# Sparse attention two heads ahead: logits, exponentials and a shorter index search in a hybrid encoder layer

## The chip, the cores and the metric

The kernel runs on one core of a Trainium2 chip. The metric is the time of one launch on the device, in microseconds; the kernel before took 3575.22 (median of 3 runs, 3574.49 to 3578.63). The engines are TensorE (PE; its weight loads are PEld), VectorE (DVE), ScalarE (ACT), GpSimd (POOL) and SyncE (SP), which issues the DMAs.

## The reference

One layer of an encoder for 2048 prompt rows and 64 sample rows (behind 512 cached ones), in float32. Normalised rows are projected into queries, keys, values and an indexer; a pooling mixer, a sparse attention (8 heads over 2 key heads, 64 wide) and an attention into 256 memory tokens (4 heads) run side by side; an output projection and a gated feed-forward with a short convolution follow. The change is in the sparse attention:

```python
s = einsum('bthd,bsd->bths', qi, ki)                  # 8 index heads of 32
score = einsum('bth,bths->bts', wi, relu(s))          # one score per query and key
score = where(visible, score, -inf)                   # chunks of 64, causal
top_val, top_idx = top_k(score, top_k)                # 256 keys of a prompt row, 144 of a sample row
...
logits = einsum('btjgd,btnjd->btjgn', qg, k_sel) * HEAD_DIM ** -0.5
p = softmax(where(valid, logits, -inf)); o = einsum('btjgn,btnjd->btjgd', p, v_sel)
```

## The kernel before, in words

The program is a row of stages (memory keys, projection, attention, then output projection and feed-forward in two halves), each ended for all engines before the next begins. The attention stage, `phase_attend`, works on 17 blocks: block n of 0 to 15 has 128 query rows and S = 128(n+1) visible columns, block 16 is the sample (64 rows, 576 columns). Columns are cut into segments of at most 512 (`segs`), tiles of 128, groups of four tiles, and units of two segments. Instead of gathering keys, the kernel finds for each row which columns belong to its largest scores and adds -1e30 to the others' logits.

For each block there are two pieces of work. First the index: TensorE multiplies index queries with index keys, a piece for each of 8 heads and each segment (`index_pieces`, L903, into the two banks of `ps_i`); ScalarE rectifies each (L1030, into a ring of three groups of four); GpSimd weighs, adds up and writes the scores (L877 to L888). VectorE then searches, row by row in parallel, a bound that leaves the wanted number above it (`pick`): it takes the smallest and largest score (L1084, L1085), halves that range 11 times, each time counting the scores above the middle (L1093) and moving it (L1096, L1097), and then takes up to eight more values below the bound by one maximum and one replacement (`take_next`, L1121 to L1124). Where a row needs more than eight, a branch (L1113) takes further rounds, and in the end a general selection by 32 rounds. Blocks 0 and 1 see at most 256 columns and need no search: there are 15.

Then the heads: 8 attention heads and one memory head a block, each a slot. TensorE makes the logits of the first two segments of the next head (`early_logits`, into the two banks of `ps_l`), then turns the present head's probabilities group by group (L946), and multiplies them with the values (L978); segments past the second come in between. VectorE adds the mask to the logits and takes the maximum, one unit at a time (`mask_logits`, L1197); ScalarE takes exponentials (L1038) and copies turned groups back to SBUF (L808); VectorE divides after heads 3, 7 and the memory head (`divide`). The memory head's exponentials are taken by ScalarE straight from `ps_l` (L1042).

The order is written out by hand, one list for each engine, over the same slots. Before the change, in slot h of block n, TensorE makes the logits of head h+1 and a tenth of the index pieces of block n+2 (a fifth in slot 8), ScalarE takes the exponential of head h+1 after all copies of head h, and VectorE does: mask of head h+1 (first unit), division, search part 2h of block n+1, mask (second unit), search part 2h+1. Each engine runs its list in order and waits on semaphores. At a block's first head TensorE waits for the exponentials of the block before, since these read `ps_l`:

```python
if h == 0 and s < 2 and b.n:
    pe.wait_ge(exp_done, NHEADS * b.n)
```

Of the kernel before, what the change touches and what calls it, by code (L numbers as in the profile page):

```python
# [12 lines left out]

# [11 lines left out]
P = 128  # L25
# [12 lines left out]
CHUNK = 64  # L38
# [10 lines left out]
HALVINGS = 11  # L49
FAR = 1.0e30  # L50
NEVER = 1.0e38
RING = 3
UNSEEN, TAKEN, TAKEN_BELOW = -2.0e38, -3.0e38, -2.5e38
# [632 lines left out]
def phase_attend(nc, t, keep):  # L686
# [10 lines left out]
    with ExitStack() as ctx:  # L697
# [9 lines left out]
        probs = m.sb("probs", [P, 2, SEQ])  # L707
# [7 lines left out]
        low, spread, back = m.sb("low", [P, 1]), m.sb("spread", [P, 1]), m.sb("back", [P, 1])  # L715
# [17 lines left out]
        KEY_LOADS, TABLE_LOADS, Q_LOADS = 6, 2, 6  # L733
        SHARE = 10
        NHEADS = NH + 1

# [19 lines left out]

        def slots():

            for b in BLOCKS:
                for h in range(NHEADS):  # L760
                    yield b, h, (b, h + 1) if h + 1 < NHEADS else (None if b.sample else (BLOCKS[b.n + 1], 0))

# [3 lines left out]
        def portion(b, part):  # L766


            total = IH * len(b.segs)
            cut = lambda part: total if part == NHEADS else total * part // SHARE  # L770
            return range(cut(part), cut(part + 1))
# [9 lines left out]
        def copy_groups(act, b, h, late=None):  # L781

            count = len(b.groups) if h < NH else 2
            for g in range(count):
                if g == 1 and late:
                    late()
                    late = None
# [22 lines left out]
            if late:  # L810
                late()
# [4 lines left out]
        def _(sp):  # L816
# [34 lines left out]
            sp.dma_start(places[:, :], t["places"]).then_inc(tables_loaded, 16)  # L851
            load(BLOCKS[1])
# [39 lines left out]
        def _(pe):  # L892
# [24 lines left out]
            def segment_logits(b, h, s):  # L917
# [8 lines left out]
                if h == 0 and s < 2 and b.n:  # L926
                    pe.wait_ge(exp_done, NHEADS * b.n)
# [21 lines left out]
            def head_values(b, h, other, numbers, after):  # L949
# [5 lines left out]
                if h < NH:  # L955
                    groups, src = b.groups, probs[0:T, seq % 2, :]
                else:
                    groups = [[(P * i, P * i + P) for i in range(4 * g, 4 * g + 4)] for g in range(2)]
                    src = probs[0:T, seq % 2, :]
# [21 lines left out]
                rest = [(*after, s) for s in range(2, len(after[0].segs))] if after and after[1] < NH else []  # L981
# [9 lines left out]
                ins.then_inc(pv_done, 1)  # L991
                for segment in rest:
                    segment_logits(*segment)

# [9 lines left out]
            early_logits(BLOCKS[0], 0)  # L1004
            for b, h, after in slots():
                other = ahead(b, 2)
                numbers = portion(other, h) if other else range(0)

                late = numbers[-1:] if h else range(0)
                if after:  # L1010
                    early_logits(*after)
                index_pieces(other, numbers[:len(numbers) - len(late)])
                if h == 0 and b.n:
                    rows_turned(BLOCKS[b.n - 1])
                head_values(b, h, other, late, after)
# [3 lines left out]
        def _(act):  # L1019
# [12 lines left out]
            def exponentials(b, h):  # L1032
# [3 lines left out]
                if h < NH:  # L1036
                    row = probs[0:T, seq % 2, 0:b.S]
                    act.activation(row, row, ACT.Exp, bias=neg[0:T, u, h:h + 1], scale=-1.0, accum_out=sums[0:T, u, h:h + 1]).then_inc(exp_done, 1)  # L1038
                    return
                act.wait_ge(turned, last_group(seq - 2) + 1)  # L1040
                for mh in range(MH):
                    ins = act.activation(probs[0:T, seq % 2, 256 * mh:256 * mh + 256], ps_l[0:T, mh // 2, 256 * (mh % 2):256 * (mh % 2) + 256],  # L1042
                                         ACT.Exp, bias=neg[0:T, u, 8 + mh:9 + mh], accum_out=sums[0:T, u, 8 + mh:9 + mh])
# [4 lines left out]
            exponentials(BLOCKS[0], 0)  # L1048
            for b, h, after in slots():
                other = ahead(b, 2)  # L1050
                numbers = portion(other, h) if other else range(0)
                early = len(numbers) - (1 if h and numbers else 0)
                if other:
                    index_relu(other, numbers[:early])
                if h == 0 and b.n:
                    copy_groups(act, BLOCKS[b.n - 1], 9)
                copy_groups(act, b, h, (lambda: index_relu(other, numbers[early:])) if other else None)
                if after:
                    exponentials(*after)
# [3 lines left out]
        def _(dve):  # L1063
            st = Steps(dve, dve_steps)

            def pick(b, part):
# [13 lines left out]
                if part == 0:  # L1080
# [7 lines left out]
                    st.step(dve.tensor_scalar(col(spread), col(mids), col(low), None, ALU.subtract))  # L1088
                    st.step(dve.tensor_scalar(steps[0:T, :], halves[0:T, :], col(spread), None, ALU.mult))
                    st.step(dve.tensor_scalar(col(mids, 1), col(mids), col(steps), None, ALU.subtract))  # L1090
# [13 lines left out]
                elif part == HALVINGS + 2:  # L1104

                    st.step(dve.scalar_tensor_tensor(low_work, low_work, -FAR, row, ALU.mult, ALU.add))
                    st.step(dve.tensor_scalar(col(place), col(above), -1.0, b.keep - 1.0, ALU.mult, ALU.add))
                    take_next(b, st, 0)
# [753 lines left out]
```

## Time and profile before

| | us |
|---|---|
| median of the runs | 3575.22 |
| the profiled execution | 3577.81 |
| its span (first to last instruction) | 3576.0 |
| TensorE matmuls busy | 3084.5 (86%) |
| VectorE busy | 2205.3 (62%) |
| GpSimd busy | 1261.6 (35%) |
| ScalarE busy | 1062.0 (30%) |

The span is the profile's time from the first to the last instruction. Busy time of an engine is the time in which at least one of its instructions ran; the idle time before an instruction is put down to what released it. The granted clock is the share of TensorE's full clock (2.4 GHz) that it was given in a stretch; its lower level is 1.2 GHz. The attention stage takes about three tenths of the span.

### The profile page before, as it was taken

What the parts mean: (1) busy time and instruction counts of PE and PEld (TensorE: products, weight loads), DVE (VectorE), ACT (ScalarE), POOL (GpSimd) and SP (SyncE); (2) the same over time, 40 slices, a digit from 0 to 9 for tenths busy, and PEclk for the clock granted to TensorE, in tenths of its full rate; (3) what the DMA queues carried; (4) which work ended last, traced back from release to release, by engine and by line L of the source; (5) the groups of instructions that cost most, each with busy time, mean ns of one, the idle gap of its engine ahead of it and who ended that gap; (6) DMA issues with size and microseconds to landing.
All of it is one profiled execution on the core that took longest, in us unless ns stands there. A gap on an engine that the chain in (4) does not pass through costs nothing. (4 is left out here: it accounts for less than half of the span.)

```text
span 3576.0 us, 49691 instructions
## 1 busy us (share of the span) xinstructions
PE 3084.5 (86%) x18810; PEld 2868.3 (80%) x18810; DVE 2205.3 (62%) x4136; ACT 1062.0 (30%) x1812; POOL 1261.6 (35%) x478
## 2 busy tenths in 40 slices
PE   3898994677778886886989999999888999999997
PEld 2777773566666775775989999999888999999996
DVE  4576672576868888863066666666512676667654
ACT  2222221444455664553122122112121212212211
POOL 0000001455666775411453343343214444434420
PEclk8999995688889997998989999999998999999998
DMA  4122225222121110003221111111132111111101
GB/s 137 70 81 78 89 84 138 56 57 57 29 57 29 29 29 26 23 14 99 78 71 36 35 59 47 35 47 47 49 103 89 36 47 59 35 35 59 47 12 50
DMA packets 164759, 201.53 MB, mean 56 GB/s; under 512 B 27759, under 2 KB 138644, under 8 KB 162580
## 3 DMA queue, kind: packets, MB, share of 16 engines
q1 hardware_dynamic: 164628, 199.86, 17.6%
q8 instruction: 73, 1.20, 0.1%
q14 instruction: 58, 0.48, 0.0%
HBM read 154.57 MB, written 45.25 MB: 56 GB/s over the span
## 5 line engine op out<-in xcount | busy, mean ns | idle before, releaser
L877 POOL TENSOR_TENSOR att_relu<-att_relu,keep_w 128x2048 f32<-128x2048 f32 (+12 forms) x84 | 255.5, 3041 | 923.0 <-ACT att_relu L1030 922.5
L1666 DVE SCALAR_TENSOR_TENSOR ffn_gv<-ffn_up,ffn_taps,ffn_gv 128x1056 f32<-128x1056 f32 (+2 forms) x264 | 417.7, 1596 | 143.0 <-ACT ffn_gv L1619 136.7
L1687 DVE TENSOR_TENSOR feed_hT<-feed_hT,ffn_ps_d 128x352 f32<-128x352 f32 x528 | 275.3, 522 | 328.4 <-PE ffn_ps_d L1572 328.4
L1559 PE MATMUL ffn_ps_u<-feed_nhi,feed_up_hi 128*128 128x352 f32 x2112 | 460.1, 326 | 15.9 <-DVE feed_nlo L1697 11.2
L1559 PE MATMUL ffn_ps_u<-feed_nhi,feed_up_lo 128*128 128x352 f32 x2112 | 456.7, 324 | 0.0
L1559 PE MATMUL ffn_ps_u<-feed_nlo,feed_up_hi 128*128 128x352 f32 x2112 | 456.0, 324 | 0.0
L1559 PEld LDWEIGHTS ffn_ps_u<-feed_nhi,feed_up_hi 128*128 128x128 f32 x2112 | 361.0, 190 | 19.7 <-DVE feed_nlo L1697 12.9
L1572 PE MATMUL ffn_ps_d<-ffn_a_hi,ffn_down_hi 128*128 128x352 f32 x1056 | 343.7, 326 | 29.3 <-DVE ffn_a_lo L1678 23.9
L1559 PEld LDWEIGHTS ffn_ps_u<-feed_nhi,feed_up_lo 128*128 128x128 f32 x2112 | 363.6, 188 | 0.0
L1559 PEld LDWEIGHTS ffn_ps_u<-feed_nlo,feed_up_hi 128*128 128x128 f32 x2112 | 360.0, 188 | 0.0
L1572 PE MATMUL ffn_ps_d<-ffn_a_lo,ffn_down_hi 128*128 128x352 f32 x1056 | 343.0, 325 | 0.0
L1572 PE MATMUL ffn_ps_d<-ffn_a_hi,ffn_down_lo 128*128 128x352 f32 x1056 | 342.6, 324 | 0.0
L978 PE MATMUL att_ps_o<-att_v,att_pT 128*128 128x128 f32 x2176 | 306.5, 291 | 35.0 <-DVE att_rows L1212 17.9
L1506 POOL TENSOR_TENSOR feed_up_hi<-feed_raw_up,feed_ones 128x1024 fp32r<-128x1024 f32 x82 | 173.1, 2111 | 460.6 <-PE ffn_ps_u L1559 460.6
L978 PEld LDWEIGHTS att_ps_o<-att_v,att_pT 128*128 128x128 f32 x2176 | 284.1, 202 | 63.9 <-ACT att_pT L808 39.1
L1626 ACT ACTIVATE ffn_a_hi<-ffn_gv 128x1056 fp32r<-128x1056 f32 x44 | 47.8, 1087 | 840.7 <-DVE ffn_gv L1676 840.7
L929 PE MATMUL att_ps_l<-att_kT,att_qa 128*128 128x512 f32 (+9 forms) x320 | 150.8, 472 | 153.0 <-ACT att_probs L1042 54.7
L808 ACT ACTIVATE att_pT<-att_ps_p 128x512 f32<-128x512 f32 (+3 forms) x370 | 193.5, 529 | 185.6 <-PE att_ps_p L946 185.0
L1093 DVE TENSOR_SCALAR_CACHE_REDUCE att_work<-att_scores,att_mids 128x384 f32<-128x384 f32 (+14 forms) x165 | 236.1, 1431 | 1.5
L1506 POOL TENSOR_TENSOR ffn_down_hi<-ffn_raw_down,feed_ones 128x2048 fp32r<-128x2048 f32 x22 | 81.2, 3689 | 425.9 <-PE ffn_ps_d L1572 425.9
L1572 PEld LDWEIGHTS ffn_ps_d<-ffn_a_hi,ffn_down_hi 128*128 128x128 f32 x1056 | 200.9, 190 | 30.2 <-DVE ffn_a_lo L1678 24.5
L1507 POOL TENSOR_TENSOR feed_up_lo<-feed_raw_up,feed_up_hi 128x1024 fp32r<-128x1024 f32 x82 | 217.1, 2648 | 6.4
(248 smaller groups left out, 6030.8 us busy)
## 6 DMA issues: line engine op xcount, KB each, us to landing
feed_raw_up<-in_w_up SPq DMA_DIRECT2D x44, 1024.0 KB, 5.0
scratch_sT<-proj_sT SPq DMA_DIRECT2D x16, 1472.0 KB, 5.1
ffn_raw_down<-in_w_down SPq DMA_DIRECT2D x22, 1024.0 KB, 4.9
feed_nlo<-scratch_mixT SPq DMA_DIRECT2D x16, 528.0 KB, 7.7
proj_x<-in_x_prompt SPq DMA_DIRECT2D x16, 512.0 KB, 4.7
att_qi<-scratch_sT SPq DMA_DIRECT2D x16, 512.0 KB, 3.8
att_qa<-scratch_sT SPq DMA_DIRECT2D x16, 512.0 KB, 5.0
att_qb<-scratch_sT SPq DMA_DIRECT2D x32, 256.0 KB, 5.6
```

Source lines behind the costliest of these rows:

```text
L808: ins = act.activation(dst, src, ACT.Copy)
L877: st.step(pool.tensor_tensor(at, at, weights, ALU.mult))
L929: pe.matmul(out, qa[:, u, h, 0:T], keys[:, h // GQ, lo:hi], start=True, stop=False)
L978: ins = pe.matmul(ps_o[0:T, P * slot:P * slot + P], pT[0:hi - lo, seq % 2, k, 0:T], values, start=first, stop=last)
L1093: st.step(dve.tensor_scalar(low_work, row, col(mids, r), None, ALU.is_gt, ALU.add, accum_out=col(counts, r)))
L1506: st.step(pool.tensor_tensor(hi, raw, ones[:, 0:1].unsqueeze(1).broadcast_to(list(raw.shape)), ALU.mult))
L1507: pool.tensor_tensor(lo, raw, hi.bitcast(F32), ALU.subtract).then_inc(ready, 1)
L1559: ins = pe.matmul(ps_u[:, half, s, 0:SUB], a[:, q, k, :], b[:, k, SUB * s:SUB * s + SUB], start=(k == 0 and n == 0), stop=(k == KC - 1 and ...
L1572: ins = pe.matmul(ps_d[:, j % 2, 0:SUB], a[:, e, P * c:P * c + P], b[:, e, SUB * s:SUB * s + SUB], start=(e == 0 and n == 0), stop=(e == 1 ...
L1626: act.activation(a_hi[:, e, :], gv[:, 1, :], ACT.Copy).then_inc(a_high, 1)
L1666: ins = dve.scalar_tensor_tensor(gv[:, half, lo:hi], up[:, lo + shift + j - 2:hi + shift + j - 2], taps[:, 2 * j + half, e:e + 1], gv[:, h ...
L1687: dve.tensor_tensor(at, at, ps_d[:, j % 2, 0:SUB], ALU.add).then_inc(partial_read[j % 2], 1)
```

## The change

Seven edits in `phase_attend` and its tables. (1) TensorE makes the logits of head i+2 in slot i, and the logits of the first two heads ahead of all slots; `probs` has three buffers in place of two, and VectorE masks head i+2 in slot i. (2) ScalarE takes the exponential of head i+1 behind the first two copies of head i, in place of all of them. (3) The memory head's logits are copied to `probs` by VectorE, and the wait quoted above is gone. (4) The search starts from mean and variance (`bn_stats`, `bn_aggr`), at the normal quantile of the wanted share, brackets 0.55 standard deviations to either side, and halves 8 times. (5) The search of block n+1 begins in slot 8 of block n-1 and its 14 parts are spread 2,2,2,2,2,1,1,2 over slots 8, 0, 1, ..., 6. (6) The index pieces of a block are made three slots earlier, in nine equal shares, two before the turns and the others one after each group's product. (7) TensorE turns the first two groups before it multiplies the first. The core of the diff:

```diff
-HALVINGS = 11
+HALVINGS = 8
+BRACKET = 0.55
-        probs = m.sb("probs", [P, 2, SEQ])
+        probs = m.sb("probs", [P, 3, SEQ])
+        SPREAD = ((0, 1), (2, 3), (4, 5), (6, 7), (8, 9), (10,), (11,), (12, 13))
+        def index_share(slot):
+            b = ahead(BLOCKS[0], (slot + INDEX_LEAD) // NHEADS + 2)
+            ...
+            total, part = IH * len(b.segs), (slot + INDEX_LEAD) % NHEADS
+            return b, list(range(total * part // NHEADS, total * (part + 1) // NHEADS))
 # copy_groups (ScalarE)
-                if g == 1 and late:
-                    late()
+                if g == 2 and exponentials:
+                    exponentials()
+                    exponentials = None
+                if g and between:
+                    between(1)
 # segment_logits and head_values (TensorE)
-                if h == 0 and s < 2 and b.n:
-                    pe.wait_ge(exp_done, NHEADS * b.n)
-                turn(0)
+                for g in range(min(2, len(groups))):
+                    turn(g)
                 for g in range(len(groups)):
-                    if g + 1 < len(groups):
-                        turn(g + 1)
-                    if g == 0:
-                        index_pieces(other, numbers)
                     if rest:
                         segment_logits(*rest.pop(0))
                     ins = multiply(g)
+                    if g + 2 < len(groups):
+                        turn(g + 2)
+                    index_pieces(other, numbers[g:g + 1])
 # pick (VectorE)
-                    dve.tensor_reduce(col(low), row, AX.X, ALU.min)
-                    st.step(dve.tensor_reduce(col(mids), row, AX.X, ALU.max))
+                    for s, (lo, hi) in enumerate(b.segs):
+                        last = dve.bn_stats(stats[0:T, s, :], row[:, lo:hi])
+                    st.step(last)
+                    st.step(dve.bn_aggr(moments[0:T, :], stats[0:T, 0:len(b.segs), :].rearrange("p s n -> p (s n)")))
+                    st.step(dve.tensor_scalar(col(sigma).bitcast(I32), col(moments, 1).bitcast(I32), 0.5, SQRT_SEED, ALU.mult, ALU.add))
                     st.step(dve.tensor_scalar(steps[0:T, :], halves[0:T, :], col(sigma), None, ALU.mult))
+                    st.step(dve.tensor_scalar(col(mids, 1), col(quantiles, b.n), col(sigma), col(moments), ALU.mult, ALU.add))
 # mask_logits (VectorE)
-                if part == 0 and seq >= 2:
-                    dve.wait_ge(turned, last_group(seq - 2) + 1)
+                if part == 0 and seq >= 3:
+                    dve.wait_ge(turned, last_group(seq - 3) + 1)
+                    dve.tensor_copy(probs[0:T, seq % 3, 0:MH * MT].rearrange("p (a n) -> p a n", a=2), ps_l[0:T, :, :]).then_inc(masked, 1)
 # VectorE's slot
-                if after:
-                    mask_logits(*after, 0)
                 if h == 0 and b.n:
                     divide(BLOCKS[b.n - 1], 2)
                 if h in (4, 8):
                     divide(b, h // GQ - 1)
+                coming, parts = pick_share(i)
+                if later:
+                    mask_logits(*later, 0)
+                for part in parts[0:1]:
+                    pick(coming, part)
+                if later:
+                    mask_logits(*later, 1)
+                for part in parts[1:]:
+                    pick(coming, part)
```

One small table more (`quantiles`) is loaded at the stage's start.

## Rows read from the trace of the kernel before

**Rows 1.** Windows by block: length, busy us (instructions) by engine, clock, DMA.
```profile
866.60:936.60 70.00, 46.61 (x264) 41.42 (x263) 47.27 (x105) 30.63 (x68) 46.60 (x19) 0.78 0.14 40
...
1201.70:1278.10 76.40, 65.65 (x409) 57.29 (x408) 61.50 (x111) 44.90 (x85) 56.35 (x22) 0.89 0.13 34
1278.10:1383.00 104.90, 68.69 (x447) 60.68 (x447) 83.48 (x136) 49.56 (x93) 65.41 (x23) 0.81 0.08 22
1383.00:1461.50 78.50, 68.17 (x472) 60.10 (x471) 68.82 (x111) 51.30 (x93) 53.68 (x17) 0.98 0.10 26
...
sum 1047.60, PE 807.96 PEld 696.83 DVE 751.77 ACT 546.16 POOL 542.94; mean PE 47.53 PEld 40.99 DVE 44.22 ACT 32.13 POOL 31.94
```
**Rows 2.** Waits in the attention stage: us in total, times, longest.
```profile
DVE att_failed L1082 <- POOL att_scores L888: 68.5, 13, 7.7
PE att_ps_l L929 <- ACT att_probs L1042: 55.4, 16, 4.9
DVE att_idle L1115 <- issue: 47.9, 13, 3.8
PE att_ps_l L929 <- DVE att_peaks L1197: 45.6, 34, 26.2
```
**Rows 3.** Timeline of VectorE, one slot of block 11: start, us, what.
```profile
1214.67 1.94 DVE L1093 TENSOR_SCALAR_CACHE_REDUCE att_work<-att_scores,att_mids 128x1664 f32<-128x1664 f32 x1
...
1217.21 1.22 DVE L1197 CUSTOM_DVE_ANT_0 att_probs<-att_ps_l,att_mask 128x1024 f32<-128x1024 f32 x1
1218.36 1.94 DVE L1093 TENSOR_SCALAR_CACHE_REDUCE att_work<-att_scores,att_mids 128x1664 f32<-128x1664 f32 x1
...
1220.91 0.75 DVE L1197 CUSTOM_DVE_ANT_0 att_probs<-att_ps_l,att_mask,att_peaks 128x512 f32<-128x512 f32 x1
1221.58 1.94 DVE L1093 TENSOR_SCALAR_CACHE_REDUCE att_work<-att_scores,att_mids 128x1664 f32<-128x1664 f32 x1
```
**Rows 4.** Timeline of TensorE in the same slots.
```profile
1216.52 1.97 PE L946 MATMUL att_ps_p<-ident,att_probs 128*128 128x128 f32 x8
...
1220.91 2.01 PE L978 MATMUL att_ps_o<-att_v,att_pT 128*128 128x128 f32 x16
...
1222.99 0.39 PE L930 MATMUL att_ps_l<-att_kT,att_qb 128*128 128x512 f32 x1
1223.22 0.40 PE L929 MATMUL att_ps_l<-att_kT,att_qa 128*128 128x512 f32 x1
```
**Rows 5.** VectorE's search by line: busy us, mean ns of one, idle before.
```profile
L1093 DVE TENSOR_SCALAR_CACHE_REDUCE att_work<-att_scores,att_mids 128x2048 f32<-128x2048 f32 x11 | 25.8, 2342 | 0.0
...
L1093 DVE TENSOR_SCALAR_CACHE_REDUCE att_work<-att_scores,att_mids 128x384 f32<-128x384 f32 x11 | 6.7, 610 | 0.2
...
L1085 DVE TENSOR_REDUCE att_mids<-att_scores 128x1 f32<-128x384 f32 (+14 forms) x15 | 20.5, 1364 | 0.0
...
L1121 DVE MAX8 att_top<-att_work 128x8 f32<-128x1792 f32 (+14 forms) x19 | 28.1, 1477 | 10.3 <-issue 6.5 <-remote 3.3
```
**Rows 6.** A copy of VectorE from PSUM: ns min/median/max, start.
```profile
L1761 DVE COPY tail_rows<-tail_ps x1: 421/421/421, 3573.3 to 3573.3; 88x256 f32<-88x256 f32 x1
```
**Rows 7.** Timeline of VectorE where block 13's search fails in a row.
```profile
1347.11 0.19 DVE L1137 TENSOR_REDUCE att_failures<-att_failedT 128x1 int32<-128x32 f32 x1
1350.54 2.03 DVE L1121 MAX8 att_top<-att_work 128x8 f32<-128x1792 f32 x1 [3.24 <-issue]
...
1376.44 0.06 DVE L1115 MEMSET att_idle<- 128x1 f32 x1 [3.48 <-remote]
```
**Rows 8.** The mask's last step at two widths, by line and shape.
```profile
L1129 DVE TENSOR_SCALAR att_mask<-att_work 128x1792 f32<-128x1792 f32 x3 | 7.3, 2432 | 0.1
...
L1129 DVE TENSOR_SCALAR att_mask<-att_work 128x2048 f32<-128x2048 f32 x1 | 1.2, 1216 | 0.0
```
**Rows 9.** Timeline of block 0: TensorE's index piece, ScalarE's copy.
```profile
614.26 0.69 PE L903 MATMUL att_ps_i<-att_kiT,att_qi 128*128 128x384 f32 x1 [3.58 <-DMA att_qi<-scratch_sT]
...
618.17 0.28 ACT L808 ACTIVATE att_pT<-att_ps_p 128x128 f32<-128x128 f32 x1 [0.56 <-PE att_ps_p L946]
```

More of the change, by code:

```diff
@@ L14 @@
+import math
 import numpy as np
@@ L809, in copy_groups @@
                 ins.then_inc(copied[e], 1)
-            if late:
-                late()
+            if exponentials:
+                exponentials()
+            if between:
+                between(2 * IH)
         block = ctx.enter_context(nc.Block())
@@ L947, in turn_group, with head_values @@
                 ins.then_inc(turned, 1)
-            def head_values(b, h, other, numbers, after):
+            def head_values(b, h, other, numbers, later):
                 u, T = b.n % 2, b.T
@@ L1003, in _ @@
             pe.wait_ge(keys_loaded, 16 * KEY_LOADS)
[L1004 to L1009, printed above, removed]
-                if after:
-                    early_logits(*after)
-                index_pieces(other, numbers[:len(numbers) - len(late)])
+            for slot in range(-INDEX_LEAD, 0):
+                index_pieces(*index_share(slot))
+            for first_heads in heads[0:2]:
+                early_logits(*first_heads)
+            for i, b, h, _, later in slots():
+                if later:
+                    early_logits(*later)
+                other, numbers = index_share(i)
+                index_pieces(other, numbers[0:2])
                 if h == 0 and b.n:
                     rows_turned(BLOCKS[b.n - 1])
-                head_values(b, h, other, late, after)
+                head_values(b, h, other, numbers[2:], later)
             rows_turned(BLOCKS[NB])
@@ L1047, in _, with relu_next @@
                 index_relu(b, range(IH * len(b.segs)))
[L1048 to L1054, printed above, removed]
+            for slot in range(-INDEX_LEAD, 0):
+                index_relu(*index_share(slot))
+            exponentials(*heads[0])
+            for i, b, h, after, _ in slots():
                 if h == 0 and b.n:
                     copy_groups(act, BLOCKS[b.n - 1], 9)
-                copy_groups(act, b, h, (lambda: index_relu(other, numbers[early:])) if other else None)
-                if after:
-                    exponentials(*after)
+                other, numbers = index_share(i)
+                def relu_next(count, other=other or b, numbers=numbers):
+                    index_relu(other, numbers[:count])
+                    del numbers[:count]
+                copy_groups(act, b, h, relu_next, (lambda: exponentials(*after)) if after else None)
             copy_groups(act, BLOCKS[NB], 9)
@@ L1219, in _ @@
             pick(BLOCKS[0], 0)
-            mask_logits(BLOCKS[0], 0, 0)
-            for b, h, after in slots():
-                if after:
-                    mask_logits(*after, 0)
+            pick(BLOCKS[1], 0)
+            for first_heads in heads[0:2]:
+                mask_logits(*first_heads, 0)
+            for i, b, h, _, later in slots():
                 if h == 0 and b.n:
@@ L1820, in program, with normal_quantile @@
         store_conv(nc, t, ident, hist)
+def normal_quantile(share):
+    lo, hi = -8.0, 8.0
+    for _ in range(60):
+        mid = 0.5 * (lo + hi)
+        lo, hi = (mid, hi) if 0.5 * (1.0 + math.erf(mid / math.sqrt(2.0))) < share else (lo, mid)
+    return lo
 def constants():
@@ L1840, in constants @@
         old.append(((s - P) > r - w)[96:] / f(w))
[L1841 removed]
+    halves = np.broadcast_to(f(BRACKET) * f(0.5) ** np.arange(HALVINGS, dtype=f), (P, HALVINGS))
+    quantiles = np.zeros((P, NB + 1), f)
+    for n, b in enumerate(BLOCKS):
+        for r in range(P):
+            seen = b.S - CHUNK if r < CHUNK and not b.sample else b.S
+            if b.keep:
+                quantiles[r, n] = normal_quantile(1 - (b.keep - 4.5) / seen)
     places = np.broadcast_to(np.arange(32, dtype=f), (P, 32))
[L1843 removed]
+    return {"halves": halves.astype(f), "quantiles": quantiles, "places": places.astype(f), "rope_table": np.concatenate(table, 1).astype(f), "band": np.array(band, f), "band_first": np.array(first, f),
             "band_old": np.array(old, f)}
```

70 lines of the change are left out of this document (33 added, 37 removed).

## The prediction

> **What bounds the kernel now.** I cut the trace by stage, then the attention stage by block. That stage runs from 606.0 to 1653.6 us of the 3576.0 us span; only it is changed, so the other 2528.4 us (and the 1.8 us by which the profiled run, 3577.81, is longer than its span) stand. In it TensorE is at work for 808 of 1047.6 us and VectorE for 752, so neither is full [rows 1]. The waits say why [rows 2]: TensorE waits on VectorE's masking (45.6 us for its running maxima alone) and, at each block's end, on the four exponentials that still read the logits' PSUM (55.4); VectorE waits for GpSimd's scores at each search's start (68.5) and on the branch that asks for failed rows (47.9, some 3.7 per search).
>
> One slot (one head) shows the loop [rows 3]. VectorE counts a halving, masks the first 1024 columns, counts another, masks 512, and begins again: 1214.67 to 1221.58, 6.91 us without a gap. Two halvings of 2.54 us and 1.83 us of masking are all of it. TensorE's work of such a slot, at the pitches of its rows at full clock (0.11 us a 128-column pass, 0.23 a 512-column one [rows 4]), is 36 passes (12 tiles, turned once, multiplied by two), six logit passes and 3.6 index passes: 4.03 + 1.37 + 0.72 = 6.1 us. In block 13, the block near full clock (0.98), this counting gives 63.7 us for all nine slots where TensorE was busy 68.2 [rows 1], so I multiply it by 1.07. So the two engines are nearly balanced, and whichever has the heavy slot sets its length.
>
> That can be tested. For each slot I took the larger of TensorE's and VectorE's sum (TensorE's divided by its block's granted clock, plus 0.65 us where one group of turned tiles leaves the copy uncovered, 0.25 where there are two), and added GpSimd's wait. Block 11 (1536 columns, searching 1664): 10.0 for slot 0 (first halving with the two reductions, a division), 7.4 three times, 7.5, 7.4, 10.8 (end of the search), 8.0 (its check), 5.5 (memory head), and 4.8 for GpSimd: 76.1 against 76.4 [rows 1]. Blocks 1 to 5, 7 to 11, 13 and 14 so come to 734.0 us against 735.0 measured. I use the same sum for the changed order.
>
> **The change, part by part.** *Eight halvings for eleven.* A count takes 0.61 us at 384 columns and 2.34 at 2048 [rows 5], so 1.04 ns a column; with its two small steps a halving is 0.80 us + 1.046 ns a column. The 15 searches have 17,600 columns together: 15 x 0.80 + 18.4 = 30.4 us a halving, 91 us for three.
> *Mean and variance for smallest and largest.* Two reductions go (20.5 us each [rows 5]), one pass of statistics per segment comes. No row shows that operation: at least one reduction's time (20.5), at most two (41) if it takes two passes. I take the lower, since it too reads one operand once, plus 0.4 us a search for the aggregate: -15 us, at worst +6. The root by one integer step and the start replace three small steps of the same size: nothing.
> *Memory head's logits copied to SBUF.* 17 copies of 1024 columns from PSUM. A copy of 256 columns took 0.42 us [rows 6]; with 1.04 ns for each further column 1024 take 1.2, at least 1.1 (no fixed part), at most 1.7 (four such copies): +20 us on VectorE (18 to 29). In return TensorE is freed by that copy, not by ScalarE's four exponentials, and two heads earlier: the 55.4 us go, and what is late next is in the slot sum.
> Together VectorE sheds 91 + 15 - 20 = 86 us, 812 to 728 by the slot sums.
> *Two heads ahead.* Masking head i+2 while TensorE multiplies head i takes masking and exponential out of the chain inside a slot. It needs a third probability buffer and adds a wait on the turns of head i-1, issued a slot earlier: free. Queued behind it on VectorE is the search, and TensorE waits for VectorE only through the next logits. TensorE's third segment of head i+2 waits for the first mask of the same slot; TensorE reaches it some 2 us after the early logits, the mask needs 1.3: covered unless VectorE's last search part runs over. So VectorE's slots of over TensorE's length still show, and a lead of about half a slot (a whole one up to 1024 columns) smooths them. I count no smoothing; it is my reserve against latencies that I can't see.
> *Index three slots earlier, search one earlier.* Scores are complete two slots sooner as seen from the search: the 68.5 us of GpSimd go. Its own work for a block (block 11's window: 56.4 us [rows 1]) stays below the new block lengths, so it becomes no bound. The qi loads have a block's time: free.
> *Exponentials behind two copies, one head ahead.* ScalarE is busy 44.9 us of block 11; copies, rectified pieces and the exponential fit in a slot. The index pieces move ahead of the turns: in blocks of one group the piece that covered the copy is gone (0.56 us of idle even now [rows 9]); in the sum.
> *Search parts.* They now sit 2,2,2,2,1,1,2,0 in slots 0 to 7 and the first two in slot 8 before, with the statistics. Slot 8 becomes VectorE-heavy (division, mask, statistics, halving: 8.5 us for block 11, beside TensorE's short memory head), slot 7 has none.
>
> Block 11 after: 8.0, five times 6.9, 9.1, 6.9, 8.5: 67.0 us, -9. Of it -4.8 is GpSimd, -2.0 slot 0, -2.8 slots 6 and 7, -2.3 the five slots between, +3.0 slot 8. TensorE stands there with its clock half-way from 0.89 to 1, because after a stall its 128-column passes take 0.21 us (1216.52, eight) and later 0.11 [rows 4], and stalls get fewer. The twelve blocks named above: 734 to 631, -103.
> *Failed rows.* Blocks 6 and 12 hold extra rounds of the search, for block 12 from 1347.11 to 1376.44, 29.3 us where 3.8 is usual [rows 7]. I worked both searches out on the reference's own scores: eleven halvings fail in one row each of the searches over 1024 and 1792 columns, by ties at zero, deep enough for one and three extra rounds, as the 19 takings of the maximum for 15 searches show [rows 5]. Eight halvings from the new start fail in the same two rows as deep, nowhere else. So 25.5 and some 8 us stay, less 3 and 4 that TensorE's lead hides: 174.9 us [rows 1] become 74.0 + 48.8 + 26.5 = 149, -25.
> *Ends.* Blocks 15 and 16 search little: -1.5. Block 0: index pieces of block 2 now stand before the first logits, and their load came at 614.26 [rows 9] after TensorE had turned two heads: +3.
> Sum: -103 - 25 - 1.5 + 3 = -126.5. Against the profiled execution 3577.81 that is 3451; against the median, 3575.22, 3449.
>
> A row that speaks against more overlap: the mask's last step took 1.22 us over 2048 columns in the last search of a prompt block, when GpSimd has no prompt block left to score, and 2.43 over 1792 [rows 8]. The Trainium skill (GPSIMD Engine Reference, section 1, Specifications) says GpSimd's SBUF interface is shared with VectorE and contends with instructions in a two-port mode or with two SBUF inputs; the trace agrees for this step. By that rule the removed counts, unhurt in every row, were the harmless part and the hurt steps stay: with GpSimd's 543 us in some 920 instead of 1048, about an eighth more of some 20 us of such delay, +3, so 3452 by the rule and 3449 without it; the sum goes without.
>
> **Rivals.** *The clock comes up whole.* Stalls gone, TensorE at 2.4 GHz throughout: the slot sum with clock 1 is 21 us lower, and with the smoothing counted another 10: 3418. For it: 0.98 in block 13 [rows 1]; against: slots 8 to 0 and the failed searches still stall. The Trainium skill (TensorE: Matmul & The Clock Gate, Part 1) says the throttled state is the default and activity releases it; the two pitches of one slot agree.
> *The lead hides little.* VectorE and TensorE still take turns, and only VectorE's 86 us come off: 3490. For it: five of nine slots of block 11 after are VectorE's or equal; against: GpSimd's 68.5 and the 55.4 are order, not work.
> *The narrow start misses.* If a row's threshold lies outside the start bracket of 0.55 standard deviations to either side, that search falls through all rounds into 31 further pairs of maximum and replacement, two passes each (a maximum over 1792 columns took 2.03 us [rows 7], a replacement the same): 124 us at 1792 columns and 25 of rounds before it, some 110 for a middling block. One block costs most of the gain, two turn it: 3449 + 2 x 110 = 3670. Against it: the counts on the reference's scores.
> Statistics at two passes (+21) and new latencies of 10 us would bring the forecast's own case to 3480.
>
> **Chances.** Forecast 0.6 (3430 to 3475), clock 0.2, little hidden 0.16, misses 0.04. Range: from a little under the clock case to over the second, 3400 to 3505. About 0.2% (7 us) can be told from no change: faster 0.93, same 0.03, slower 0.04.
>
> **What would show it.** Right: VectorE's wait for GpSimd at the search's start near nothing; no TensorE wait on exponentials at a block's end; block 11 near 67 us with 6.9 us slots; 120 counts for 165; still 19 takings of the maximum; block 12 still long, near 97. Wrong: VectorE gap-free over whole blocks with TensorE still waiting for its peaks (second case); further takings of the maximum (third); statistics of over 1.1 ns a column; ScalarE's rectified pieces waiting for GpSimd.

## The result: 3510.4 us, faster by half of the forecast

The changed kernel took 3510.38 us (median of 4, 3508.38 to 3515.71); before took 3576.07 beside it: ratio 0.9819, interval 0.9807 to 0.9831. That is -66 us for a forecast of -126.5, 5 us above the range. The profiled span fell from 3576.0 to 3509.8, all of it in the attention stage: it ends at 1587.2 instead of 1653.6, and 1922.6 us follow where 1922.4 did. Blocks of the kernel after, in the columns of [rows 1]:
```profile
1149.97:1219.47 69.50, 61.24 (x411) 54.18 (x410) 53.09 (x105) 43.25 (x85) 56.95 (x21) 0.95 0.13 37
1219.47:1325.29 105.82, 67.44 (x446) 61.03 (x446) 79.96 (x130) 46.80 (x93) 60.56 (x21) 0.82 0.08 22
1325.29:1410.79 85.50, 70.55 (x465) 63.66 (x465) 66.58 (x104) 46.49 (x89) 60.37 (x20) 0.90 0.09 24
...
sum 981.18, PE 759.77 PEld 669.57 DVE 706.28 ACT 517.18 POOL 551.28; mean PE 44.69 PEld 39.39 DVE 41.55 ACT 30.42 POOL 32.43
```
Block 11 came near its forecast (69.5 for 67.0), but partly by luck: its slot 0 took 14.1 us where the forecast had 8.0, its slot 8 5.0 where it had 8.5. Block 12 did not move, and block 13 got longer, 78.5 to 85.5, its clock down from 0.98 to 0.90. The waits, as in [rows 2]:
```profile
PE att_ps_l L944 <- DVE att_peaks L1218: 71.6, 39, 28.5
PE att_ps_l L944 <- DVE att_neg L1218: 55.2, 20, 11.0
DVE att_idle L1136 <- issue: 46.6, 13, 3.8
PE att_ps_o L993 <- ACT att_pT L822: 41.8, 94, 0.8
...
DVE att_failed L1099 <- POOL att_scores L905: 1.4, 1, 1.4
```
GpSimd's 68.5 us at the search's start are gone, and so is TensorE's wait on the memory head's exponentials, 55.4. TensorE's wait on the running maxima, which should have shrunk, grew from 45.6 to 71.6. VectorE's groups by line (busy us, mean ns), beside [rows 5, 6, 8]:
```profile
L1113 DVE TENSOR_SCALAR_CACHE_REDUCE att_work<-att_scores,att_mids 128x384 f32<-128x384 f32 (+14 forms) x120 | 171.7, 1431 | 1.0
L1150 DVE TENSOR_SCALAR att_mask<-att_work 128x1792 f32<-128x1792 f32 (+14 forms) x18 | 47.9, 2660 | 0.1
L1126 DVE SCALAR_TENSOR_TENSOR att_work<-att_work,att_scores 128x384 f32<-128x384 f32 (+14 forms) x15 | 40.0, 2666 | 0.0
L1142 DVE MAX8 att_top<-att_work 128x8 f32<-128x1792 f32 (+14 forms) x19 | 28.0, 1473 | 10.2 <-issue 6.9 <-remote 3.3
L1103 DVE BATCH_NORM_STATS2 att_stats<-att_scores 128x6 f32<-128x512 f32 (+10 forms) x40 | 22.1, 606 | 0.0
...
L1208 DVE COPY att_probs<-att_ps_l 128x1024 f32<-128x1024 f32 (+1 forms) x17 | 20.6, 1214 | 0.0
...
L1109 DVE TENSOR_SCALAR att_steps<-att_halves,att_sigma 128x8 f32<-128x8 f32 (+1 forms) x15 | 8.5, 568 | 0.5
```
Counts, statistics, copy and the 19 maxima are as forecast. Three other rows grew though they do the same work. In the kernel before they read:
```profile
L1129 DVE TENSOR_SCALAR att_mask<-att_work 128x1792 f32<-128x1792 f32 (+14 forms) x18 | 31.9, 1770 | 0.1
L1106 DVE SCALAR_TENSOR_TENSOR att_work<-att_work,att_scores 128x384 f32<-128x384 f32 (+14 forms) x15 | 26.1, 1741 | 0.2
L1089 DVE TENSOR_SCALAR att_steps<-att_halves,att_spread 128x11 f32<-128x11 f32 (+1 forms) x15 | 4.1, 272 | 0.5
```
So the mask write went from 31.9 to 47.9 us, the step that leaves out what is above the bound from 26.1 to 40.0, and a small step at the search's start from 4.1 to 8.5.

**Where the miss sits.** A slot ends with TensorE's last product of its head. Summed over the forecast's twelve ordinary blocks (us), with block 12, blocks 1 to 16 together, and the median time (the forecast's row is its slot sum; what stands on record of it is the 631 and the slots of block 11):
```
                               slots 1-5   6+7     8      0    all  block 12   1 to 16    time
before                           369.2  115.0  150.6  100.0  734.8   104.9  1017.3    3576.1
forecast                         309.1  163.2   81.2   77.6  631.1    96.5              3449
after                            313.3  169.7   90.3  110.0  683.3   105.8   941.2    3510.4
e1  search a slot earlier        313.0  168.4  109.6   80.3  671.3   102.4   926.3    3494.6
e2  end split                    331.2  143.4   65.3  129.5  669.4   108.7   943.2    3505.2
e3  mask in count form           312.7  163.7   77.0  118.9  672.3   103.8   927.0    3489.9
e4  eleven halvings              315.1  200.7   89.5  110.3  715.6    89.7   962.6    3531.1
e5  search alone, end early      372.5  150.6  119.3  102.8  745.1   111.7  1032.6    3594.4
e13 search alone                 356.1  128.9  111.5  104.3  700.8   103.8   993.8    3548.9
e16 order alone                  317.8  204.3   88.0  133.9  744.0   103.8  1006.8    3571.0
e6  halving out of slot 8        307.6  185.6   88.4   90.8  672.4   100.9   926.6    3497.9
e7  mask write accumulating      313.8  157.6   76.6  116.9  664.9   105.9   921.1    3487.9
e8  GpSimd in halves             312.5  161.3   78.7  113.1  665.6   107.3   924.9    3493.6
e9  e6 + e7                      309.0  164.9   74.5   95.3  643.7    98.9   894.2    3461.2
e10 e6 + e7 + e8                 309.9  160.1   76.5   91.3  637.8    98.6   888.2    3452.0
e11 e10, additions halved        311.0  158.3   77.4   92.9  639.5    99.1   890.6    3454.6
e12 e7 + e8, end split           310.2  154.4   67.3   93.4  625.3    96.6   871.9    3438.6
e14 exponentials last            307.0  167.8   90.2  108.8  673.8   104.5   931.1    3495.8
e15 before, accumulating write   372.7  113.8  146.8  100.9  734.3   105.1  1018.8    3573.5
e17 e12 + e14                    309.8  153.4   68.8   83.2  615.2    96.3   862.2    3426.3
```
Of the 52 us that the twelve blocks are over, 32 are slot 0's, 9 slot 8's, 6.5 slots 6 and 7's; blocks 6 and 12 add 11, block 0 7, and blocks 15 and 16 give 9 back. Block 0 isn't compared: in these profiles the stage's first keys landed anywhere from 584.5 to 592.1 us, whatever the edit. Some us of a difference in time can come from there, so the column for blocks 1 to 16 is the better measure of an edit.

**Slots 8 and 0 add up.** VectorE at the end of block 10 (start, us):
```profile
1144.91 0.18 DVE L1228 RECIPROCAL att_inv<-att_sums 128x4 f32<-128x4 f32 x1 [4.23 <-PE att_ps_o L993]
...
1147.67 1.56 DVE L1103 BATCH_NORM_STATS2 att_stats<-att_scores 128x6 f32<-128x416 f32 x3
...
1152.08 1.94 DVE L1113 TENSOR_SCALAR_CACHE_REDUCE att_work<-att_scores,att_mids 128x1664 f32<-128x1664 f32 x1
...
1154.84 0.62 DVE L1237 TENSOR_TENSOR att_rows<-att_ps_o,att_inv 128x64 f32<-128x64 f32 x4
```
and TensorE in the same stretch:
```profile
1152.22 0.50 PE L944 MATMUL att_ps_l<-att_kT,att_qa 128*128 128x512 f32 x1 [2.25 <-DVE att_neg L1218]
...
1155.52 1.54 PE L961 MATMUL att_ps_p<-ident,att_rows 128*128 128x128 f32 x6 [1.70 <-DVE att_rows L1237]
...
1157.41 1.94 PE L961 MATMUL att_ps_p<-ident,att_probs 128*128 128x128 f32 x8 [0.35 <-ACT att_rowsT L822]
```
VectorE stands idle 4.23 us in slot 7 until TensorE has finished head 7, then works through division, mask, statistics and a halving. TensorE's slot 0 first waits 2.25 us for a mask behind the statistics, then 1.70 us for the memory head's division (1154.84), which comes only behind the halving. TensorE resumes at 0.24 us a pass, near the slower pitch of [rows 4].

**The burst in slots 6 and 7, and the port.** VectorE some slots earlier:
```profile
1127.26 1.22 DVE L1208 COPY att_probs<-att_ps_l 128x1024 f32<-128x1024 f32 x1
1128.39 4.51 DVE L1150 TENSOR_SCALAR att_mask<-att_work 128x1536 f32<-128x1536 f32 x1
...
1137.13 0.06 DVE L1136 MEMSET att_idle<- 128x1 f32 x1 [3.40 <-issue]
1137.27 1.22 DVE L1218 CUSTOM_DVE_ANT_0 att_probs<-att_ps_l,att_mask 128x1024 f32<-128x1024 f32 x1
```
GpSimd in the same stretch:
```profile
1128.35 3.73 POOL L900 TENSOR_TENSOR att_relu<-att_relu 128x1664 f32<-128x1664 f32 x1
1132.16 2.54 POOL L902 TENSOR_TENSOR att_relu<-att_relu 128x832 f32<-128x832 f32 x1
```
The write began 0.04 us after GpSimd's addition and ended 0.82 us after it: 4.51 = 3.69 + 0.82, and 0.82 is about its price unhurt, by the 1216 ns for 2048 columns of [rows 8]. The next mask came late, and TensorE waited:
```profile
1138.56 0.79 PE L944 MATMUL att_ps_l<-att_kT,att_qa 128*128 128x512 f32 x1 [4.77 <-DVE att_peaks L1218]
```
It goes the other way too. VectorE in block 12:
```profile
1259.58 5.46 DVE L1126 SCALAR_TENSOR_TENSOR att_work<-att_work,att_scores 128x1792 f32<-128x1792 f32 x1
```
and GpSimd there:
```profile
1258.87 4.29 POOL L900 TENSOR_TENSOR att_relu<-att_relu 128x1920 f32<-128x1920 f32 x1
1263.24 3.89 POOL L902 TENSOR_TENSOR att_relu<-att_relu 128x960 f32<-128x960 f32 x1
```
The same addition, some 16 us earlier:
```profile
1247.59 2.24 POOL L902 TENSOR_TENSOR att_relu<-att_relu 128x960 f32<-128x960 f32 x1
```
VectorE waited for the first addition and ran 1.88 us, to 1265.04; the second addition, begun under it, took 3.89 us where 2.24 is its price. The Trainium skill (SBUF — State Buffer, section SBUF: two separate sides) calls the port pair that the two engines share an exclusive lock, held for a whole instruction by whichever starts first; the trace agrees in both directions.

### The profile page after: what moved, and what is told of

It reads as the page before. It is cut to its first block and busy times, and to the rows that moved or that the text cites. A ratio compares the mean times of both kernels' runs of the same rounds, so it can differ in the third digit from the quotient of the medians.

```text
span 3509.8 us, 49568 instructions
## 1 busy us (share of the span) xinstructions
PE 3040.6 (87%) x18810; PEld 2845.3 (81%) x18810; DVE 2147.9 (61%) x4013; ACT 1033.0 (29%) x1812; POOL 1269.0 (36%) x478
## 5 line engine op out<-in xcount | busy, mean ns | idle before, releaser
L894 POOL TENSOR_TENSOR att_relu<-att_relu,keep_w 128x2048 f32<-128x2048 f32 (+12 forms) x84 | 256.1, 3048 | 833.2 <-ACT att_relu L1047 833.0
L993 PE MATMUL att_ps_o<-att_v,att_pT 128*128 128x128 f32 x2176 | 309.4, 288 | 46.6 <-ACT att_pT L822 38.0
L944 PE MATMUL att_ps_l<-att_kT,att_qa 128*128 128x512 f32 (+9 forms) x320 | 142.5, 446 | 132.8 <-DVE att_peaks L1218 71.6
L536 PE MATMUL proj_ps_g<-proj_whi,proj_xhi 128*128 128x512 f32 (+5 forms) x544 | 192.1, 353 | 18.2 <-DVE proj_wlo L579 15.5
```

The lines of the kernel that those rows point to most:

```text
L536: ins = pe.matmul(ps_g[0:T, g, 0:b - a], p[:, c, 0:T], q[:, c, a:b], start=(c == 0 and k == 0), stop=(c == KC - 1 and k == 2))
L894: st.step(pool.tensor_tensor(at, at, weights, ALU.mult))
L944: pe.matmul(out, qa[:, u, h, 0:T], keys[:, h // GQ, lo:hi], start=True, stop=False)
L993: ins = pe.matmul(ps_o[0:T, P * slot:P * slot + P], pT[0:hi - lo, seq % 2, k, 0:T], values, start=first, stop=last)
```

## Experiments

Behind each expectation stands the median time in us, with its ratio to the kernel before beside it and the 95% interval of the ratio. Gains are told against the kernel after ("after"), in e5, e13, e15 and e16 against before. The edits are shown shortened.

**Where the time went (e1 to e4).** Theories: slots 8 and 0 in series; the burst at the search's end; the port; VectorE's work.
```diff
-after: SPREAD = ((0, 1), (2, 3), (4, 5), (6, 7), (8, 9), (10,), (11,), (12, 13))
+e1: SPREAD = ((0, 1), (), (2, 3), (4, 5), (6, 7), (8, 9), (10,), (11,), (12, 13)), started in slot 7 (slot + 2)
+e2: SPREAD = ((0, 1), (2, 3), (4, 5), (6, 7), (8, 9), (10, 11), (12,), (13,))
-e3: dve.tensor_scalar(mask, work, -0.5 * FAR, MASKED, is_gt, mult)
+e3: dve.tensor_scalar(mask, low_work, -0.5 * FAR, None, is_gt, add, accum_out=back)
-e4: HALVINGS = 8
+e4: HALVINGS = 11, SPREAD = ((0, 1), (2, 3), (4, 5), (6, 7), (8, 9), (10, 11), (12, 13), (14, 15, 16))
```
e3 leaves the mask's values out: ones and zeros are added to the logits.

> The changed kernel with one edit: the search's first two parts (statistics, first halving) move from slot 8 to slot 7, where VectorE idles; slot 8 gets none. Theory (the division behind the memory head is queued behind the search parts of slot 8, and TensorE's slot 0 follows that division in series instead of beside it): slot 0 of the 12 ordinary blocks 1 to 14, 110 us in the changed kernel against 78 forecast, falls to about 80; the time falls by 25 to 35 us, to about 3480. Rival (slot 0 is long because TensorE's clock is down and rows have to be turned and copied, whatever VectorE does): within 8 us of 3510.

3494.62 us (ratio 0.9767, 0.975 to 0.9783): 16 us less than after, not the 25 to 35 of the theory. Slot 0 fell by 30 us, nearly its whole miss, so what stood ahead of the memory head's division made it long. But slot 8 gave 19 back, and the two together fell by only 10. Slot 8 holds no part of the search now; there TensorE waits for masks that stand behind slot 7's parts in VectorE's list, as in block 10 (the mask behind the halving):
```profile
1146.41 0.50 PE L944 MATMUL att_ps_l<-att_kT,att_qa 128*128 128x512 f32 x1 [1.76 <-DVE att_peaks L1218]
```

> The changed kernel with one edit: the end of the search is spread over slots 4, 5 and 6 (one taking of the maximum earlier, mask earlier, only the branch left in slot 6). Theory (a burst of VectorE work in slot 6, longer than TensorE's lead, holds TensorE's third segment in slot 7): the sum of slots 6 and 7 of the 12 ordinary blocks, 170 us, falls by 15 to 25 and the time with it, to about 3490. Rival (slots 6 and 7 came out near the forecast, 170 against 163, so the burst is covered): within 7 us of 3510.

3505.16 (0.9794, 0.9778 to 0.9811): the rival's size. Slots 6 and 7 fell by 26 us as the theory said and slot 8 by 25, but slots 0 to 5 took 37 back and blocks 6, 12 and 16 another 16; block 16 took 39.5 us for 28.9, at a granted clock of 0.65 that stays unexplained. The mask writes fell as well, from 47.9 us:
```profile
L1150 DVE TENSOR_SCALAR att_mask<-att_work 128x1792 f32<-128x1792 f32 (+14 forms) x18 | 28.4, 1577 | 0.1
```
So e2 doesn't separate the burst from the port; in e12, where the write is unhurt, the split takes 6 us off slots 6 and 7.

> The changed kernel, with the step that writes the mask at a search's end in the form of the counts (one operand, with an accumulator); it writes 1 and 0 in place of -1e30 and 0, so the mask is left out of the logits. Theory (that step runs in VectorE's two-port form and waits for the end of the GpSimd instruction under way): its 15 first calls take 1.05 ns a column as the counts do, some 20 us together in place of 41, and the time falls by 5 to 20 us. Rival (the step is long for another reason, such as what it writes): its calls stay at 2.7 us each and the time stays.

3489.91 (0.9758, 0.9741 to 0.9774): the port theory. The write fell to 1365 ns each, the time by 20.5 us, of which blocks 1 to 16 show 14.

> The changed kernel with 11 halvings in place of 8 (same start, same order); the three more move the end of the search later, so that slots 4 and 5 carry two heavy parts and slot 6 three. Forecast's terms: VectorE has 91 us more; by the larger of the two engines per slot the time rises by 50 to 60 us, to about 3565. Rival (two heads of lead hide the search, and the halvings were worth little): under 15 us more.

3531.1 (0.9866, 0.985 to 0.9883), +20.7, between the two. Its search needs fewer further rounds, which its maxima show (19 after), so block 12 is 16 us shorter; without that three halvings cost some 37 us.
```profile
L1142 DVE MAX8 att_top<-att_work 128x8 f32<-128x1024 f32 (+14 forms) x17 | 23.8, 1403 | 6.5 <-issue 6.5
```

**Each half of the change alone (e5, e13, e16).** e5 and e13 are before with the new search in place of the old; e16 is after with the old search's start and halvings.
```diff
 e5:  pick(ahead(b, 1), 2 * h); mask_logits(*after, 1); pick(ahead(b, 1), 2 * h + 1), as before
+e13: the parts of after's SPREAD[h] in slots 0 to 7 instead of 2 * h and 2 * h + 1
-e16: bn_stats, bn_aggr, sigma
+e16: tensor_reduce min, tensor_reduce max; HALVINGS = 11 and SPREAD as in e4
```

> The order of before, with the new search alone (mean and variance, eight halvings). From the run with eleven halvings in the new order (3531 us) the three halvings are worth 21 us there, and so the order alone 45 us of the 66. Theory (the lead hides much of what DVE does, so in the old order the same DVE time stands more openly in the chain): clearly more than 21 us is won here, 45 to 65 us, so 3511 to 3531 us, and the two edits together are worth less than the sum of each alone. Rival (the two add up): 21 us, about 3555 us.

3594.41 (1.0052, 1.0034 to 1.007): 19 us slower than before, against both theories. With fewer parts, two to a slot, the mask write and the branch fell into slot 6: slots 6 and 7 took 36 us more and slot 8 31 less.

> The order of before with the new search, its last step kept in slot 7 as before had it (the run e5 ended it a slot earlier and came out 19 us slower than before). Theory (in the old order slots 1 to 5 are a chain from logits to products in which DVE's search only fills idle time, so the halvings are worth little there; e5 lost by moving the burst): between 0 and 15 us faster than before, 3560 to 3576 us. Rival (the new search itself costs time in that order, at its start or by GpSimd): again 10 us or more slower, about 3590 us.

3548.91 (0.9919, 0.9903 to 0.9936): 30 us faster than before, more than the theory had, and in spite of a block 16 that took 47.2 us instead of 33.3, at a granted clock of 0.54 that I can't explain.

> The new order alone, with the search of before whole (minimum, maximum and eleven halvings). Theory (the lead carries most of the gain, the lighter search some 21 us on top by the run with eleven halvings, and one more reduction a search makes 15 us of DVE more): 3531 to 3545 us. Rival (the order alone leaves DVE's slots the bound, the gain of each part is half): about 3550 us or more.

3571.0 (0.9976, 0.9965 to 0.9986): the rival; the order alone is worth 8 us. So the two halves take off 8 and 30 us alone and 66 together. With the old search slots 6, 7 and 0 take back all that slots 1 to 5 and 8 win. That it packs three parts into slot 6 is a part of this that I did not separate.

**Terms of the miss taken away, singly and together (e6 to e12).**
```diff
+e6:  SPREAD = ((0,), (1, 2), (3, 4), (5, 6), (7, 8), (9, 10), (11,), (12, 13))
+e7:  dve.tensor_scalar(mask, work, -128.0 / FAR, None, mult, add, accum_out=back)
+e8:  for two in (slice(0, 2), slice(2, 4)): pool.tensor_tensor(at[:, two], at[:, two], weights[:, two], mult)
+e11: e10, and GpSimd's tensor_tensor(last_four, first_four, last_four, add) in two halves as well
+e12: e7, e8 and SPREAD = ((0,), (1, 2), (3, 4), (5, 6), (7, 8), (9, 10), (11, 12), (13,))
```


> After, with the first halving moved from slot 8 to slot 0 and every later step by one place, (0,), (1, 2), (3, 4) and so on to (9, 10), (11,), (12, 13). Theory (slots 8 and 0 stand in series: what DVE does in slot 8 puts off the memory head's division and with it PE's slot 0): slots 8 and 0 together lose a halving a block, 1 to 2 us by 12 blocks, some 15 us, and slots 4 and 5 give back a third of it, since they are PE's: about 3500 us. Rival (the series comes from the order of the division alone, or the halving is only moved on to the next slot, which waits as much): within 4 us of 3510.

3497.85 (0.9783, 0.9766 to 0.9799), the theory's size by another sum: slot 0 -19, slots 6 and 7 +16, slot 8 hardly moved. The mask writes rose to 51.6 us and the left-out step fell from 40.0 to 29.6, so this edit too changes what meets GpSimd.

> After, with the mask written in the accumulating form of TENSOR_SCALAR as in the run with the count form, but with the mask whole: each place that is chosen gets +128 and each other place about 0, from one multiplication by -128e-30. Theory (the write in the two-port form waits for the end of GpSimd's instruction and the accumulating form doesn't): 15 writes fall from 2.7 us to about 1.37 us each, and the time falls as it did with the count, to about 3490 us. Rival (the gain of that run came from the mask of zeros and ones): about 3510 us.

3487.86 (0.975, 0.9733 to 0.9766): the theory, with a whole mask. VectorE's rows fell by 22.2 us (47.9 less 25.7), the time by 22.5, blocks 1 to 16 by 20:
```profile
L1150 DVE TENSOR_SCALAR_CACHE_REDUCE att_mask<-att_work 128x1792 f32<-128x1792 f32 (+14 forms) x18 | 25.7, 1428 | 0.1
```


> After, with GpSimd's weighing of four heads in two instructions of two heads each. Theory (a two-port DVE instruction waits for the end of the GpSimd instruction that runs): the longest wait falls from 3.7 us to about 1.9 us, so the mask writes and the write of the left-out scores fall from 48 and 40 us to about 38 and 32 us in all, and the time by 5 to 12 us, to about 3500 us, though GpSimd gets longer by the fixed cost of one more instruction a group. Rival (what matters is how much GpSimd works in all): the DVE rows don't fall, and the time stays at 3510 us or rises.

3493.63 (0.9771, 0.9754 to 0.9787): more than expected; the mask writes fell to 36.3 us, the left-out step to 35.0. Half as long a GpSimd instruction hurts less, though GpSimd's weighing rose from 256.1 to 274.2 us.

> The shifted search (run with the halving moved out of slot 8, -12.5 us against 3510.4) and the mask written in the accumulating form (-22.5 us) together. Theory (they are two different terms, one in slots 8 and 0, one in slots 6 and 7): they add, 3470 to 3480 us. Rival (both only give DVE room at the block's end, where the same wait is cut by either): less than 5 us under the better of the two, 3483 to 3488 us.

3461.19 (0.968, 0.9664 to 0.9697): 49 us, more than the 35 of the two alone (47 and 35 in blocks 1 to 16).

> The two of the run before this one and GpSimd's weighing in halves. Theory (the mask write no longer meets the port; what is left for shorter GpSimd instructions is the write of the left-out scores and the small steps at the search's start, 35 and 9 us of DVE in the run with the halves, against about 23 and 4 unhurt): 3 to 8 us more than without the halves, about 3468 us. Rival (the halves give what they gave alone, 17 us, by another way than the mask write): about 3458 us.

3452.03 (0.9661, 0.9645 to 0.9677): 9 us more than e9, between the two.

> As the run before, with GpSimd's adding of the two weighed fours in halves as well (42 instructions of 3.95 us become 84 of about 2 us). Theory (the wait is for the end of the running GpSimd instruction, so its longest bound is what counts): the DVE rows of the left-out scores and of the small steps fall again, the time by 2 to 6 us. Rival (little is left to win, and GpSimd's scores come later): the same within 2 us, or slower.

3454.58 (0.9656, 0.9639 to 0.9672): the rival, no difference from e10.

> The mask in the accumulating form, GpSimd's weighing in halves, and the search put as (0,), (1, 2), (3, 4), (5, 6), (7, 8), (9, 10), (11, 12), (13,): the mask write beside MAX8 in slot 5, the branch alone in slot 6. Theory (slots 6 and 7 pay for a burst of two parts behind which the next head's masking waits; with the write unhurt and the branch alone the burst is cut): slots 6 and 7 fall by 10 to 20 us against the third run of this call, slots 1 to 5 take some of it back, about 3462 us. Rival (the burst only moves by a slot): within 3 us of 3468.

3438.56 (0.9615, 0.9599 to 0.9631), better than expected, but by other slots: against e10 slots 6 and 7 fell by 6 us (10 to 20 expected) and slot 8 by 9, and slots 1 to 5 took nothing back, as they had in e2. Its blocks 11 to 13:
```profile
1110.96:1179.24 68.28, 60.92 (x410) 53.28 (x410) 55.24 (x107) 43.19 (x85) 57.55 (x29) 0.98 0.14 37
1179.24:1275.86 96.62, 63.93 (x446) 58.51 (x446) 74.89 (x133) 46.76 (x93) 61.39 (x29) 0.86 0.09 24
1275.86:1347.12 71.26, 64.63 (x466) 58.31 (x465) 59.20 (x104) 46.26 (x89) 61.30 (x27) 1.00 0.11 29
```
Block 13 is 14 us shorter than after's; VectorE's busy time there fell by 7, and the granted clock rose from 0.90 to 1.00. Why the edits are worth more together stays open. One reading is that a stall that goes also brings passes back to 2.4 GHz. Another is that an edit alone moves the search into other meetings with GpSimd, but that gives some 4 of the 14 us that e9 has beyond e6 and e7: the write that it frees took 51.6 us in e6 and 47.9 in after, and the left-out step is as in e6 (29.4 for 29.6).

**The rest (e14, e15, e17).** e15 is before with e7's write; e17 is e12 with e14's edit, which puts the exponentials behind all copies:
```diff
-                if g == 2 and exponentials:
-                    exponentials()
-                    exponentials = None
```

> After, with the next head's exponentials behind all copies of turned groups instead of behind the first two (a change only from block 8 on, where there are three groups or more). Theory (they run a head ahead, so the place costs nothing, and the copies come sooner): within 5 us of 3510. Rival (PE waits on exponentials at each turn again): 10 to 25 us slower, about 3530 us.

3495.82 (0.9769, 0.9752 to 0.9785): 15 us faster, against both theories; blocks 1 to 16 show 10 of them. TensorE's wait for turned copies falls from 41.8 us:
```profile
PE att_ps_o L990 <- ACT att_pT L819: 32.5, 75, 0.7
```
The exponential, a head ahead, has no hurry; the copies that it held up have. The mask writes fell too, from 47.9 to 42.0 us, so some of it may be the port's.

> Before, with its mask write in the accumulating form. In its trace the 18 writes take 31.9 us; unhurt in this form they take 25.7 us. Theory (the meeting with GpSimd is mostly of the new order's making): within 6 us of before, 3570 to 3576 us. Rival (the form is worth 20 us in any order): about 3555 us.

3573.46 (0.9987, 0.9978 to 0.9997): the theory. In the old order the write's form is worth some 5 us (1 to 8 by the interval); in the profiles blocks 1 to 16 take 1018.8 us for 1017.3, so none of it shows there.

> The run with the split end of the search (3438.6 us) with the exponentials behind all copies, which alone took 14.6 us off after. Theory (the copies come sooner for TensorE's products in each slot of blocks 8 to 14, whatever the search does): 8 to 15 us less, about 3427 us. Rival (the gain came from another meeting of the mask write with GpSimd, which is gone here): within 4 us of 3438.6.

3426.28 (0.9583, 0.9565 to 0.9602): 12 us less. Its first keys landed 7 us sooner, but blocks 8 to 11 are shorter by 9 too, so the place counts without the mask write's meetings. It beats both kernels, before by 150 us and after by 84.

## Why the prediction was wrong

- **The step that failed:** "I use the same sum for the changed order". The larger of two engines is a slot's length only where neither waits for the other within it. In the old order the sum had been tested on whole blocks; in the new one the search's start stands ahead of the mask and the division that TensorE's slot 0 waits for. Slots 8 and 0 add up: 200 us where the sum had 159. e1 brought slot 0 to 80, near the forecast's 78, but moved part of the wait on to slot 8; only with the halving out of slot 8 and the mask write unhurt as well did the two come near the forecast's size (170 in e9, 161 in e12, 152 in e17).
- **The port, priced +3 and left out of the sum:** the price was an eighth of a delay read off before, but the delay is the rest of a GpSimd instruction, and the new order moved VectorE's steps into more of them. Against their unhurt prices (0.59 ns a column from 1216 ns for 2048 [rows 8], for 22,208 columns; 1.05 from the 1.88 us above, for 17,600) the two large steps lost some 26 us before and 56 after. By e3 and e7 the mask write alone cost 20 to 22 us of the time (14 and 20 in blocks 1 to 16); in the old order the same edit gave some 5 (e15).
- **"Covered unless VectorE's last search part runs over":** it ran over, by write and branch (1128.39 to 1137.27), and TensorE's third segment waited 4.77 us. I had named the condition and not worked it out: 1.22 + 4.51 + 4.16 us stand before that mask.
- **The exponential's place:** "copies, rectified pieces and the exponential fit in a slot" priced it at nothing. It cost 10 to 15 us (e14), since ScalarE's fit says nothing of who waits for its copies.
- **Held:** the three halvings' size, the statistics at one reduction's price (22.1 us for 20.5), the copy (1214 ns for 1.2 us), GpSimd's and the exponentials' waits, the two failed searches, and slots 1 to 5 (313 for 309). e4 adds that only part of the halvings' 91 us was ever on the path.
- **The rivals:** "the lead hides little" gave the nearest time, 3490, but not its mechanism: VectorE is busy 53.1 of block 11's 69.5 us, and with the new search the order is worth 38 us (e13 to after), some 14 of them e13's unexplained block 16. The clock didn't come up whole; in e12 it nearly did, and the time went under the forecast.

## What to carry to other kernels

Before using a slot sum on a new order, walk each engine's queue over the boundary between two blocks: whatever stands ahead of the instruction that the other engine waits for is added, not overlapped. Price each VectorE step that meets GpSimd by the rest of the GpSimd instruction under way, and look for a form of it that is not hurt. When an engine's work is put ahead, what it used to precede becomes urgent: place that first.

## What the hardware showed

- VectorE's accumulating TENSOR_SCALAR ran at its own pace beside GpSimd in the runs shown (1428 ns mean for the mask, 2075 for 1792 columns counted), while the same engine's plain TENSOR_SCALAR waited 3.69 us in block 10. So the slower form is the faster one here, though a count of 2048 columns takes 2342 ns [rows 5] and an unhurt plain write 1216 [rows 8].
- Even a step of 128x8 elements waited: 1.30 us at 1149.76 in block 10, where 0.27 was the mean before. It ended at 1151.06, as GpSimd's instruction did:
```profile
1147.86 3.17 POOL L894 TENSOR_TENSOR att_relu<-att_relu,keep_w 128x1792 f32<-128x1792 f32 x1 [8.89 <-ACT att_relu L1047]
```
- The branch on failed rows costs 3.4 to 3.8 us of idle VectorE each time, much as before (46.6 us in 13, 47.9 before).
